# Expert values of 192 tokens summed from gathered rows of V, the other 384 by dense matmuls

## What is computed

```python
experts = jnp.take_along_axis(cidx, top_p, axis=-1)      # (N, 8, 16) numbers of experts
gate = jax.nn.softmax(top_s, axis=-1)
act = jax.nn.gelu(jnp.einsum('nd,nhkd->nhk', h, u[experts]).astype(jnp.float32), approximate=False)
return jnp.einsum('nhk,nhkd->nd', (gate * act).astype(h.dtype), v[experts])
```

## Time and profile before

| what | value |
|---|---|
| median of 3 runs | 5255.22 us (5254.07 to 5256.73) |
| profiled execution, its own time | 5250.18 us |
| its span, first to last instruction | 5248.4 us |
| mean granted TensorE clock | 0.989 of full |
| TensorE busy | 5130.6 us, 98% |
| VectorE / ScalarE / GpSimd busy | 2908.5 / 1248.6 / 1091.0 us |
| expert value stage | 3566.8 to 5208 us |

### The profile page before, as it was taken

One profiled execution on the slowest core, in us unless ns is written; L12 is line 12 of the kernel. 1 busy time (PEld: TensorE's weight loads), 2 busy tenths in 40 slices (PEclk: granted clock), 3 DMA queues, 4 the chain that ended last, 5 costly groups with the idle time before them and its releaser, 6 DMA issues.

```text
span 5248.4 us, 98470 instructions
## 1 busy us (share of the span) xinstructions
PE 5130.6 (98%) x39847; PEld 5045.1 (96%) x39847; DVE 2908.5 (55%) x5530; ACT 1248.6 (24%) x1527; POOL 1091.0 (21%) x554
## 2 busy tenths in 40 slices
PE   8999999999998999999999999999999999999998
PEld 8999899889998999999999999999999999999997
DVE  3323632323436687888888886334555555555555
ACT  3222533321212122222222222112211111122112
POOL 1010023210000000000110110004444444444441
PEclk9999999999999999999999999999999999999999
DMA  6333257644453344455565555444444444334442
GB/s 192 96 109 91 64 190 248 219 143 126 122 156 78 70 105 107 103 122 138 131 144 133 134 143 129 108 135 143 125 125 132 130 133 128 125 125 125 125 132 78
DMA packets 574527, 677.54 MB, mean 129 GB/s; under 512 B 183633, under 2 KB 413009, under 8 KB 556632
## 3 DMA queue, kind: packets, MB, share of 16 engines
q1 hardware_dynamic: 531344, 527.72, 36.1%
q0 software_dynamic: 37440, 136.33, 8.9%
q10 hardware_dynamic: 5520, 10.49, 0.7%
HBM read 563.22 MB, written 106.72 MB: 128 GB/s over the span
## 4 chain that ended last, share of the span: by engine, by line
PE 96%; DVE 2%; ACT 1%; issue 1%; DMA 0%; ACTq 0%; DVEq 0%
PE pair L1665 57%; PE pair L2070 31%; PE pair L1629 2%; PE pair L2022 1%; PE pair L1836 1%; ACT w_hi L699 1%; PE pair L1701 1%; PE pair L1879 1%; PE pair L1976 0%; PE pair L1780 0%; PE pair L1751 0%; DVE tmp L1125 0%; PE pair L1936 0%; DVE x_in L1079 0%; PE pair L1801 0%
## 5 line engine op out<-in xcount | busy, mean ns | idle before, releaser
L1665 PE MATMUL pair<-act_hi,w_hi 128*128 128x288 f32 x7616 | 1652.6, 299 | 32.9 <-DVE act_lo L1129 11.9
L1665 PE MATMUL pair<-act_hi,w_lo 128*128 128x288 f32 x7616 | 1635.2, 296 | 0.0
L1665 PE MATMUL pair<-act_lo,w_hi 128*128 128x288 f32 x7616 | 1634.0, 296 | 0.0
L1665 PEld LDWEIGHTS pair<-act_hi,w_hi 128*128 128x128 f32 x7616 | 1227.4, 189 | 71.8 <-issue 64.6
L1665 PEld LDWEIGHTS pair<-act_lo,w_hi 128*128 128x128 f32 x7616 | 1231.2, 189 | 0.0
L1665 PEld LDWEIGHTS pair<-act_hi,w_lo 128*128 128x128 f32 x7616 | 1231.1, 189 | 0.0
L1582 DVE TENSOR_TENSOR main<-pair,main 128x576 f32<-128x576 f32 x1024 | 775.7, 757 | 785.3 <-PE pair L2070 785.3
L2070 PE MATMUL pair<-wx_hi,v_hi 128*128 128x288 f32 x4096 | 878.2, 296 | 9.7 <-DVE wx_lo L1576 9.7
L2070 PE MATMUL pair<-wx_hi,v_lo 128*128 128x288 f32 x4096 | 878.2, 296 | 0.0
L2070 PE MATMUL pair<-wx_lo,v_hi 128*128 128x288 f32 x4096 | 878.0, 296 | 0.0
L2070 PEld LDWEIGHTS pair<-wx_hi,v_hi 128*128 128x128 f32 x4096 | 661.1, 189 | 9.9 <-issue 9.9
(11 more groups left out here) (265 smaller groups left out, 3340.9 us busy)
## 6 DMA issues: line engine op xcount, KB each, us to landing
w_raw<-in_peer_u_dram SPq DMA_DIRECT2D x512, 256.0 KB, 5.3
v_raw<-in_peer_v_dram SPq DMA_DIRECT2D x128, 1024.0 KB, 5.5
w_raw<-in_w_in_dram SPq DMA_DIRECT2D x64, 1024.0 KB
gelu_dram<-tmp SPq DMA_DIRECT2D x128, 288.0 KB, 2.5
gmat_dram<-gmat POOLq DMA_DIRECT2D x36, 1024.0 KB, 11.3
a_back<-gelu_dram SPq DMA_DIRECT2D x128, 288.0 KB, 5.8
g_back<-gmat_dram SPq DMA_DIRECT2D x128, 288.0 KB, 6.2
w_raw<-in_w_out_dram SPq DMA_DIRECT2D x16, 1024.0 KB
```

Of the source, the lines that this page charges most:

```text
L1665: op = m_(pair[out][:, hf, 0:TH], w[:, k, :], x[:, k, hf * TH:(hf + 1) * TH], start=(starts and k == ks[0] and i == 0), stop=(ends and k = ...
```

## The change

The last 192 tokens leave the dense stage. `TV` = 384 tokens stay: the dense matmuls become one of 384 columns for each two of 288 (`bank(d)`: four banks of PSUM, so that pairs 2 and 3 of PSUM are free). The gate matrices are made for 48 groups in place of 72.

For the 192 tokens VectorE works out for each chosen expert the cell of `gelu_dram` (`e_cell`) and the row of V (`e_row`). A batch is four tokens. For each token GpSimd issues one indirect DMA that gathers its 128 rows of V (1 MB, into `e_rows`, 8 buffers, so two batches) and one that gathers its 128 GELU values (4 bytes each, into `e_act`); it multiplies these with the gates into a 128 x 4 column set of the otherwise zero `e_w` [128, 4, 32]. TensorE then makes 16 unsplit fp32 matmuls of 512 columns (4 column groups x 4 quarters of the channels), which add the four tokens to row c of each quadrant of PSUM; 32 batches fill the quadrants (block 0), the other 16 are block 1. A batch runs inside `value_sums` ahead of block d = 4 of one pair: batches 0 to 31 in pairs 8 to 39, batches 32 to 47 in pairs 42 to 57. In pairs 40 and 58 the sums of a block are turned by 16 transposes (`turn_expert_sums`), after ScalarE has copied them to `e_rows[7]`, and VectorE adds them to `main` in 8 additions.

`wx` is now made by VectorE (`weigh`), for the pair after the next inside `value_pair`; GpSimd keeps v_lo of all tiles and does the gathers. The semaphores `u_in` and `v_in` are folded into `raw_in`, and the squares of the final norm get buffers of their own.

```diff
-N_G = T // NTOK_G
+TV = 384
+N_SP = T - TV
+N_G = TV // NTOK_G
+SP_BLOCKS = ((0, 32, 8), (32, 16, 42))
...
+            def bank(d):
+                return pair[d % 4 // 2][:, d % 2, 0:TV]
...
+            for p in range(1, N_U // 2):        # GpSimd
+                value_low(2 * p)
+                value_low(2 * p + 1)
+                if p == 2:
+                    for s in range(2):
+                        pool.wait_ge(a_out[s], 16 * N_U // 2)
+                    for b in range(2):
+                        gather_rows(b)
+                    for b in range(4):
+                        gather_cells(b)
+                if p == 4:
+                    for b in range(2):
+                        weigh(b)
+                if p - 1 in SP_PAIR:
+                    b = SP_PAIR[p - 1]
+                    pool.wait_ge(e_mm, b + 1)
+                    if b + 2 < N_BATCH:
+                        weigh(b + 2)
+                        if b + 2 == SP_BLOCKS[0][1] + 1:
+                            pool.wait_ge(e_turned, 2)
+                        gather_rows(b + 2)
+                    if b + 4 < N_BATCH:
+                        gather_cells(b + 4)
...
+            def gather_rows(b):
+                for j, t in enumerate(batch_tokens(b)[0]):
+                    pool.indirect_dma_start(out=e_rows[b % 2 * COLS + j][:, :], out_offset=None, in_=v_rows,
+                                            in_offset=bass.IndirectOffsetOnAxis(ap=e_row[:, t:t + 1], axis=0)
+                                            ).then_inc(e_in[b % 2][j], 16)
...
+            def weigh(n, s):                     # VectorE
+                dve.wait_ge(ag_in[s], (n - s) * 16 + 32)
+                v.tensor_tensor(wx[s][:, :], a_back[s][:, :], g_back[s][:, :, :].rearrange("p b t -> p (b t)"), ALU.mult).then_inc(wx_val, 1)
+            def value_pair(n, i, last=False):
                 for m in range(2):
                     dve.wait_ge(wx_hid, n + (m + 1))
+                    v.tensor_sub(wx_lo[i + m][:, :], wx[m][:, :], wx_hi[i + m][:, :].bitcast(F)).then_inc(wx_lod, 1)
+                if not last:
+                    for m in range(2):
+                        dve.wait_ge(wx_lod, n + (m + 1))
+                        weigh(n + (2 + m), m)
...
+            def expert_sums(b, s, m, first=False):   # TensorE
+                pe.wait_ge(e_wval, b * 2 + 2)
+                for j in range(COLS):
+                    pe.wait_ge(e_in[s][j], m * 16 + (16 + E_IN))
+                for c in range(4):
+                    for j in range(COLS):
+                        op = m_(pair[2 + c // 2][quadrant(j), c % 2, :], e_w[s][:, j, :],
+                                e_rows[s * COLS + j][:, c * 512:(c + 1) * 512], start=first, stop=True, skip_group_check=True)
+                op.then_inc(e_mm, 1)
...
-                        for hf in range(2):
-                            op = m_(pair[d % 4][:, hf, 0:TH], w[:, c], x[:, hf * TH:(hf + 1) * TH],
-                                    start=(j == 0), stop=(j == 5))
+                        op = m_(bank(d), w[:, c], x[:, :], start=(j == 0), stop=(j == 5))
```

More of the change, by code:

```diff
@@ L58 @@
 G_FIRST = SEL_TILES * TB
-N_G = T // NTOK_G
+TV = 384
+N_SP = T - TV
+N_G = TV // NTOK_G
 GB = 64
+SP_BLOCKS = ((0, 32, 8), (32, 16, 42))
+N_BATCH = sum(nb for _, nb, _ in SP_BLOCKS)
+SP_PAIR = {pair + i: first + i for first, nb, pair in SP_BLOCKS for i in range(nb)}
+SP_TAKE = {pair + nb: k for k, (_, nb, pair) in enumerate(SP_BLOCKS)}
 NQ, QR = 4, 32
@@ L343, in raw_count, with batch_tokens @@
             return 16 * n
+        U_RAW = [raw_count(N_W - 2 + s) for s in range(2)]
+        V_RAW = [U_RAW[s] + 16 * NQ * N_U // 2 for s in range(2)]
+        e_in = (vp_in, kp_in)
+        E_IN = 16 * DB * PAGES // V_RING
+        CELLS_IN = [16 * (2 + 8 + (8 if s < 2 else 0)) for s in range(4)]
+        def batch_tokens(b):
+            first, nb, _ = next(x for x in SP_BLOCKS if x[0] <= b < x[0] + x[1])
+            return [COLS * first + nb * j + b - first for j in range(COLS)], b - first
+        def bank(d):
+            return pair[d % 4 // 2][:, d % 2, 0:TV]
         def page_of(n):
@@ L664, in _, with value_low, gather_cells @@
[L664 to L668 removed]
+            def value_low(n):
+                pool.wait_ge(v_hid, n + 1)
+                g.tensor_tensor(v_lo[n % 4][:, :], v_raw[n % 2][:, :], v_hi[n % 4][:, :].bitcast(F), ALU.subtract).then_inc(v_lod, 1)
+            def gather_cells(b):
+                for t in batch_tokens(b)[0]:
+                    pool.indirect_dma_start(out=e_act[:, t:t + 1], out_offset=None, in_=gelu_cells,
+                                            in_offset=bass.IndirectOffsetOnAxis(ap=e_cell[:, t:t + 1], axis=0)
+                                            ).then_inc(back_in[b % 4], 16)
@@ L1581, in take_sums, with add_expert_sums @@
                     dve.wait_ge(acc_ps, at + (d + 1))
-                    v.tensor_add(as_halves(main[:, d, :]), halves(d % 4), as_halves(main[:, d, :])).then_inc(acc_done, 1)
-            FRONT, BACK = range(12), range(12, KD)
-            value_pair(0, 0, True)
+                    v.tensor_add(main[:, d, 0:TV], bank(d), main[:, d, 0:TV]).then_inc(acc_done, 1)
+            def add_expert_sums(k):
+                first, nb, _ = SP_BLOCKS[k]
+                at = TV + COLS * first
+                for i in range(2):
+                    dve.wait_ge(e_turned, 2 * k + i + 1)
+                    out = main[:, 8 * i:8 * i + 8, at:at + COLS * nb].rearrange("p k (j c) -> p k j c", c=nb)
+                    ps = turned_x(pair[2 + i], P).rearrange("p k (j c) -> p k j c", c=QR)[:, :, :, 0:nb]
+                    for j in range(COLS):
+                        op = v.tensor_add(out[:, :, j, :], ps[:, :, j, :], out[:, :, j, :])
+                    op.then_inc(e_added, 1)
+            FRONT, BACK = range(12), range(12, KD)
+            dve.wait_ge(a_done, N_U)
+            for m in range(2):
+                dve.wait_ge(v_hid, m + 1)
+                v.tensor_sub(v_lo[m][:, :], v_raw[m][:, :], v_hi[m][:, :].bitcast(F)).then_inc(v_lod, 1)
+                weigh(m, m)
+            value_pair(0, 0)
             dve.wait_ge(hT_back, 16)
             take_sums(0, FRONT)
-            value_pair(2, 2, True)
+            value_pair(2, 2)
             dve.wait_ge(hT_back, 32)
```

180 lines of the change are left out of this document (123 added, 57 removed).

## The result

The changed kernel takes 5329.2 us (median of 4 runs, 5313.0 to 5342.0) against 5256.0 (4 runs, 5254.1 to 5257.1) for the kernel before beside it: ratio 1.0138, 95% interval 1.0104 to 1.0172. It is 1.4% slower; 4948 was forecast. The profiled execution took 5318.8 us, its span is 5316.7, its mean granted TensorE clock 0.953.

The account below looks back on a forecast made before the run. TensorE's matmuls were taken to bound the value stage (1641.0 us), forecast at 1356.5: -284.5, with gate matrices -22.8 making -307.3. From 5250.2 that gives 4942.9, plus 5.0 for the median: 4948 us, range 4866 to 5080.

Parts of the forecast that it names:

- g's small pieces I take as a bit worse off than even: T = 21.2 us: Value stage: g shares DMA engines with gathered rows slightly worse than evenly, making each pair with a batch 21.2 us.
- rows all went first: Bound on g's landing: the rows (4.19 MB, 9.8 us) all pass before the remaining load, giving T = 24.5 us.
- `weigh` at 0.5 us: VectorE's `value_pair`: making `wx` ahead of the take of block 12 costs 0.5 us.
- The half clock at 5 us: TensorE after long stalls runs at half clock: 1.7 us lost each, 5 us for the three large stalls.
- Dense pairs, T = 17.8: Value-stage pairs without a batch take 17.8 us, held by a two-pair loop through g's landing, not 16.66.
- GpSimd "just hidden": GpSimd's work in a batch pair needs T >= 19.7 us, just hidden; a gather dearer by 0.3 us would show.
- The stalls outside the pattern: Value-stage extras: 23 us at p = 2, 18 around pair 40, 3.5 first pair, 2 pair 58, 5 half clock.
- TensorE's work: Value stage: 384-column matmuls of 173.5 ns, 16.66 us a pair; a batch 3.6 us, so 20.3 with a batch.
- slower: the four groups don't overlap: Rival: column groups don't overlap at 512 columns, batch 14.5 us, total 5428; chance 0.07 shared with slow rows.
- TensorE keeps its beat: Rival: landings come earlier and the loops never bite, pairs of 20.3 and 16.66 us, total 4866; chance 0.15.
- the other slower case: Rival: gathered rows drained under 256 GB/s make the kernel slower; chance 0.07 shared with batches not overlapping.
- GpSimd or the rows' transfer holds the batch pairs: Rival: GpSimd's time or the 8 KB rows hold batch pairs at T = 24, total 5082; chance 0.21.

Follow-up runs that it names:

- Kernels 1: Changed kernel with only gmat_dram's layout altered, so g comes in 128 pieces of 1536 bytes in place of 768: 5123.0 us, ratio 0.9754 to the kernel before.
- kernel 2: Changed kernel with only SyncE's order altered: a and g of both tiles issued once `wx` has read the old ones, ahead of v: 5010.3 us, ratio 0.9532.
- kernel 9: Changed kernel plus g in larger pieces, weights ahead of v, cell gathers before rows, starting gathers spread, rows gathered two by two: 4842.2 us, ratio 0.9230.
- kernel 3: Changed kernel with both g in 1536-byte pieces and a and g issued ahead of v: 5007.4 us, ratio 0.9531 to the kernel before.
- kernels 8 to 11: Four kernels on two later chips; 8, 9, 10 have lines. The last: changed kernel with only kernel 9's GpSimd gather edits, loads unchanged: 5145.0 us, 0.9806.
- kernel 8: Kernel 3 with the cell gathers of all batches after the fourth left out, row gathers kept: 4868.4 us, ratio 0.9279 to the kernel before.
- kernel 10: Changed kernel with each v_lo of GpSimd split into four instructions of 512 columns: 5254.1 us, ratio 1.0012 to the kernel before.

## Why the prediction was wrong

- **The step that failed**: "g's small pieces I take as a bit worse off than even: T = 21.2 us". A batch pair took 28.6. The loop was the right one, in the right order (v_hi, v_lo, load, g, `weigh`, take of block 12), and its first part was exact: g issued 12.5 us into the pair. The landing was wrong. I shared the engines by bytes, even at worst, and bounded it by "rows all went first"; the engines share by pieces, which puts 768 of 256 bytes against 8 KB rows at one row each: 17.5 us from issue to landing. The pairs took 48 x (28.6 - 21.2) = 355 us of the 363 by which the stage missed its forecast. Kernels 1 and 2 show it: with g in larger pieces a batch pair takes 24.6 us, with g out of the way of the rows 23.0. The 5.6 us between 28.6 and 23.0 hold the next two points as well, which follow from the landing.
- **`weigh` at 0.5 us**: mis-sized where it lies beside a v_lo, up to 4.7 us. I priced the move of `wx` to VectorE by its size alone, though v_lo stayed on GpSimd and a late g moves `wx` right onto it. The 24 long ones took 73 us too much, in the same stalled pairs; what of that reached the total time is not shown.
- **The half clock at 5 us**: mis-sized. I charged it for three stalls; it comes behind every stall. In the stretch of 960 us TensorE was busy 750.6 us, 22.3 us for each of its 33.6 pairs in place of 20.3: 2 us a pair, an estimated 95 of the 355 us. It vanishes with the stalls (clock 1.00 in kernel 9).
- **Dense pairs, T = 17.8**: 21.6 where they stalled (half of 43.3), by `wx` and the clock again.
- **GpSimd "just hidden"**: right in the kernel after, which waits 213.3 us for the batch. Missing were the late signals of TensorE while GpSimd issues gathers. They are in the trace of the kernel after (90 takes of the batch pairs over 0.3 us late) and may explain most of what kernels 2 and 3 still had over TensorE's 20.45 us, 2.5 us a pair. Their cause is open.
- **The stalls outside the pattern**: at p = 2 the number was right by luck: pairs 1 and 2 took 17.2 + 40.8 = 58.0 us, 58.1 forecast. The 24 gathers took 29.7 us (29.9), but VectorE stalled one pair earlier than I had it: a g issued at 3585.45, just as the burst of rows began, landed at 3610, and `wx` waited 22.5 us for it while the gathers ran beside. It is the failed step again, not v_lo behind the gathers. Pairs 40 and 41 took 26.1 + 30.4, forecast 36 + 17.8.
- **TensorE's work**: right. 384 columns every 0.17 us, a batch 3.64 us (3.6), so the rival "slower: the four groups don't overlap" did not decide, nor the other slower case: rows drained at 416 GB/s, not under 256. "GpSimd or the rows' transfer holds the batch pairs" foresaw too little (24) and the wrong holder. The gain itself is real: "TensorE keeps its beat", forecast at 4866, 389 us less than before, is what kernel 9 does, 4842.2 against 5246.4, 404 less: on a chip without late signals.

The mistake of direction was to give the slower side only mechanisms of TensorE and of bytes. The loop had 0.7 us of room under TensorE's 20.3 us, so, beyond 1.4 us, every us of g's landing counted half, and I had no row for small pieces beside 8 KB rows.

## What to carry to other kernels

When a stage gets shorter, list the small transfers whose landing was hidden by its length, and issue them ahead of the big ones, as soon as their buffer is free: here 4.7% faster in place of 1.4% slower hung on the place of a 192 KB load (kernel 2). Where a transfer in small pieces runs beside one in large pieces, count pieces on each queue, not bytes. Before an element-wise step is moved between VectorE and GpSimd, look what the other runs at that moment: shorter instructions of GpSimd kept VectorE's `wx` short, though the time that this alone saves was not separated. And when two kernels are compared over several experiments, check that something that neither edit touches looks the same in both: here an unchanged burst of gathers gave away that more than the edit differed.

## What the runs showed of the hardware

- DMA engines with work on two queues took one 256-byte piece and one 8 KB row in turn (53 and 49 in a us, 416 GB/s together; kernel after, 4014 to 4020).
- With 8 KB rows the engines moved 400 to 424 GB/s from 4014 to 4020 in the kernel after, and 345 GB/s for 600 us in kernel 9 beside a fully busy TensorE.
- A gather of 128 pieces costs GpSimd 0.94 us + 0.30, whether a piece is 4 bytes or 8 KB.
- While GpSimd issued gathers, TensorE's signals reached VectorE up to 5.2 us late in the batch pairs of kernel 3, and up to 23.6 us late in its burst of 24. On two other chips (kernels 8 to 11) none was late, not in the same burst (kernel 8) and not with eight gathers in a row (kernel 10). The cause stays open.
- An idle TensorE of 12.4 us was followed by 6 us at a granted clock of 0.60, so mostly at 1.2 GHz of its 2.4.
- `wx` with two operands from SBUF took up to 4.69 us in place of 0.55 beside v_lo of GpSimd; all 24 long ones ended 0.41 or 0.42 us behind the end of a v_lo.
